# Squaring each block right behind its clipping on ScalarE, in the feed-forward stages of a fused transformer kernel

## The reference

```
def squared_relu_mlp(h, w1, w2):
    return jnp.square(jax.nn.relu(h @ w1)) @ w2
```

## Time and profile before

| | us |
|---|---|
| median of 3 runs | 3998.24 (3997.82 to 4001.41) |
| the profiled execution, its own time | 3994.2 |
| its span, first to last instruction | 3992.4 |
| TensorE matmul busy | 3734.4 (94%) |
| TensorE weight load busy | 3000.8 (75%) |
| VectorE busy | 1972.5 (49%) |
| ScalarE busy | 1335.9 (33%) |
| GpSimd busy | 807.8 (20%) |

### The profile page before, as it was taken

The page is one execution under the profiler, slowest core; times in us unless marked ns, Lnnn a source line. Parts: engine busy times, 40 slices in busy tenths (PEclk is TensorE's granted clock), DMA queues, the critical chain, the costliest instruction groups (busy, mean ns, idle before and its releaser), DMA issues. The chain is left out here.

```text
span 3992.4 us, 54790 instructions
## 1 busy us (share of the span) xinstructions
PE 3734.4 (94%) x20683; PEld 3000.8 (75%) x20683; DVE 1972.5 (49%) x2905; ACT 1335.9 (33%) x2365; POOL 807.8 (20%) x604
## 2 busy tenths in 40 slices
PE   6998899999999899999999999999989988899998
PEld 4775688888878677777776688888878865577886
DVE  5736643333353564333446663333356638746445
ACT  3346532121243454222335422121233324433222
POOL 1500012222122111222220012222110018701222
PEclk9999999999999999999999999999999989999999
DMA  5134223233221212444310023233211230032222
GB/s 177 64 116 127 64 85 120 91 112 109 86 73 63 76 42 85 153 152 149 106 55 1 12 89 124 87 118 103 91 56 63 76 118 14 19 106 94 92 91 71
DMA packets 191734, 352.34 MB, mean 88 GB/s; under 512 B 41980, under 2 KB 43597, under 8 KB 191565
## 3 DMA queue, kind: packets, MB, share of 16 engines
q1 hardware_dynamic: 183789, 333.48, 25.5%
q10 hardware_dynamic: 7792, 16.78, 1.1%
HBM read 341.71 MB, written 16.92 MB: 90 GB/s over the span
## 5 line engine op out<-in xcount | busy, mean ns | idle before, releaser
L568 POOL TENSOR_TENSOR x<-x,scaled_buf 128x512 f32<-128x512 f32 (+1 forms) x360 | 465.3, 1298 | 2296.6 <-DVE scaled_buf L560 2295.9
L129 DVE TENSOR_TENSOR w_lo<-raw,w_hi 128x2048 fp32r<-128x2048 f32 x198 | 459.1, 2319 | 789.3 <-ACT w_hi L123 774.9
L123 ACT ACTIVATE w_hi<-raw 128x2048 fp32r<-128x2048 f32 x197 | 377.1, 1914 | 1206.3 <-PE psum L385 1203.9
L383 PE MATMUL psum<-hT_hi,w_hi 128*128 128x256 f32 (+1 forms) x1920 | 677.8, 353 | 3.1 <-issue 1.7
L384 PE MATMUL psum<-hT_lo,w_hi 128*128 128x256 f32 (+1 forms) x1920 | 674.5, 351 | 0.0
L385 PE MATMUL psum<-hT_hi,w_lo 128*128 128x256 f32 (+1 forms) x1920 | 674.1, 351 | 0.0
L383 PE MATMUL psum<-w_hi,uT_hi 128*128 128x512 f32 x1280 | 505.7, 395 | 17.7 <-DVE uT_lo L639 17.7
L560 DVE TENSOR_TENSOR scaled_buf<-psum,gate 128x512 f32<-128x512 f32 x360 | 246.6, 690 | 512.3 <-PE psum L385 478.7
L385 PE MATMUL psum<-w_hi,uT_lo 128*128 128x512 f32 x1280 | 499.3, 390 | 0.0
L384 PE MATMUL psum<-w_lo,uT_hi 128*128 128x512 f32 x1280 | 498.9, 390 | 0.0
L383 PE MATMUL psum<-w_hi,hT_hi 128*128 128x512 f32 x1072 | 420.6, 392 | 9.3 <-ACT qkv L1232 5.9
(11 more groups left out here) (277 smaller groups left out, 4742.9 us busy)
## 6 DMA issues: line engine op xcount, KB each, us to landing
mod_wide<-in_w_mod SPq DMA_DIRECT2D x24, 3072.0 KB, 10.6
raw<-in_w_mlp SPq DMA_DIRECT2D x64, 1024.0 KB, 5.2
raw<-in_ff_w SPq DMA_DIRECT2D x64, 1024.0 KB, 5.3
raw<-in_ssm_w_in SPq DMA_DIRECT2D x20, 1024.0 KB, 5.1
mod_slab<-in_w_mod SPq DMA_DIRECT2D x8, 2048.0 KB, 8.0
raw<-in_b_w_qkv SPq DMA_DIRECT2D x12, 1024.0 KB, 5.1
raw<-in_a_w_qkv SPq DMA_DIRECT2D x11, 1024.0 KB, 5.1
mod_first<-in_w_mod ACTq DMA_DIRECT2D x4, 2048.0 KB, 17.0
```

The source lines that it names most:

```text
L123: act.activation(K.w_hi[h][:, :, :], K.raw[h][:, :, :], ACT.Copy).then_inc(K.hi_done.h, 1)
L129: dve.tensor_tensor(K.w_lo[h][:, :, :], K.raw[h][:, :, :], K.w_hi[h][:, :, :].bitcast(F32), ALU.subtract).then_inc(K.lo_done.h, 1)
L383: pe.matmul(out, hi_a, hi_w, start=first, stop=False, **check)
L568: pool.tensor_tensor(x, x, K.scaled_buf[:, j % 2, :], ALU.add).then_inc(K.added.h, 1)
```

## The change

The squaring of bank j is issued directly behind the clipping of bank j. Before, it was issued behind the clipping of bank j+1 (and the last one behind the squaring ahead of it). The same instructions with the same waits remain; their order on ScalarE changes from clip 0, clip 1, square 0, clip 2, square 1, ... to clip 0, square 0, clip 1, square 1, ...

```
                     tile_done(act, c, 0, j)
                     act.wait_ge(K.sq_done.h, sq0 + nt * c + j - 1)
                     act.activation(K.relu[:, j % 2, :], K.bank[j][:, :], ACT.Relu).then_inc(K.relu_done.h, 1)
-                    if j:
-                        square(c, j - 1)
-                square(c, nt - 1)
+                    square(c, j)
                 split_hi(K, act, g + 1, 1)
```

## The result

| | us |
|---|---|
| before, median of 4 runs | 3998.03 |
| with the change, median of 4 runs | 3974.38 (3972.85 to 3976.63) |
| ratio | 0.9941, 95% interval 0.9929 to 0.9953 |
| profiled execution, own time, before and after | 3994.2 and 3973.86 |
| its span, before and after | 3992.4 and 3972.0 |

The kernel is 0.59% faster, 23.6 us in the medians (18.8 to 28.4 by the interval), 20.3 us between the two profiled executions. Forecast were 22.2 us and a time of 3976.0 with a range of 3969 to 3986.

The account below looks back on a forecast made before the run. TensorE, running matmuls 94% of the span, was taken to bound the kernel, stalling for block 2 in sixteen chunks. Removing 16 x 1.386 = 22.2 us from the median 3998.24 gave 3976.0 us, 8-in-10 range 3969 to 3986.

Parts of the forecast that it names:

- The place: Sixteen chunks of the stages without context: TensorE waits for block 2 of `uT_lo`; stages with context: cost and gain 0.
- The cause: On ScalarE, square 2, data ready since 1636.81, stands behind clipping 3, which waits for bank 3, and starts at 1639.43.
- The size: TensorE in each stalled chunk: 1.386 us lost by matmul starts, 1.41 by chunk length; 16 x 1.386 = 22.2 us.
- The two counts by idle time: TensorE's wait for `uT_lo`: 17.7 us by matmul rows, 24.4 by weight loads, taken to bracket the stall's size.
- What is late next: Stages without context: block 3 reaches TensorE at 1641.42, is wanted at 1642.75, so 1.3 us to spare.
- the cover: Down-projection start: 18 matmuls, k = 0 to 2 of two tiles, 4.1 us, hide the line's 2.8 us.
- The hand-over from a clipping to its square: ScalarE, from a clipping's end to its dependent square: 0.03 us, with 0.1 as the other end.
- The slab half and the first gating: VectorE: half 1's subtraction over at about 1644.4, wanted at 1649.5; first gating waits for it, at no cost.
- The slower rival: ScalarE loses its clip-square overlap, 0.13 x 160 = 21 us, and becomes the pace: 4019 us; chance 3%.
- The new wait of a square for VectorE: ScalarE: a square waits for VectorE's block j-2 ahead of the next clipping; square 2 has 3.4 us to spare.
- Given back in part: Shift against reduced-clock dips, or block 3 later than worked out, leaves half the gain: 3987 us; chance 7%.
- the shift that the rival spoke of: All that follows the shortened chunks moves by 11 and 22 us against the clock's dips; part of the 7% rival.

Follow-up runs that it names:

- fivefold square: New order, with square 3 computed five times in the sixteen chunks without context tokens, against the kernel before: 3995.79 us, ratio 1.0001.
- taking the cover away: New order, but TensorE takes all four products of output tiles 0 and 1 at once, against the kernel before: 3985.33 us, ratio 0.9974.
- the fourth experiment: ScalarE in old order; TensorE takes k = 0 and 1 of output tiles 0 and 1 before k = 2, against the kernel before: 3976.80 us, ratio 0.9949.

## Why the prediction was right

- *The place.* TensorE waits for block 2, in the sixteen chunks of the stages without context, and nowhere else. Shown: the new order there alone gives all, with context tokens it gives nothing, and square 2 alone gives all.
- *The cause.* Square 2 stood behind clipping 3, whose data came later. Shown twice, from both sides: by moving that square and by letting TensorE ask later.
- *The size.* 1.386 us a chunk by starts, 1.41 by the length of six chunks. Measured 1.41 by the chunks' length (44.935 to 43.52), 22.6 us for sixteen. The medians moved by 23.6, the profiled executions by 20.3; both hold 22.2 within what runs of one kernel differ by (3.8 us among the four of the changed one). The two counts by idle time, 17.7 and 24.4, would have been off by 4.9 and 1.8 us from the chunks' length: the matmul rows leave out the slow step behind a gap and part of the gap itself.
- *What is late next.* Block 3, with 1.3 us to spare, from the rows of before. In the profile after it is 1643.08 - 1641.73 = 1.35, less 0.05 on the way. The fivefold square gives 1.31, and taking the cover away exposed the line at the size worked out (0.74 us late, 0.7 expected).
- *The hand-over from a clipping to its square* was taken as 0.03 us with 0.1 as the other end. Both occur: 0.03 (1636.56 to 1637.19) and 0.11 (1633.84 to 1634.55). It touched nothing, since both fit in the idle 1.38 us ahead of the next clipping.
- *The slab half and the first gating.* VectorE's subtraction of the half ends at 1642.38 + 2.29 = 1644.67, that is 5.67 us behind the start of the down-projection, where 5.7 were worked out (1644.4 against 1638.66). TensorE had no wait from it. The first gating does stand behind it, as forecast, and starts at 1644.59. In its sum for the end of tile 0 the prediction counted one step too many: the 21st matmul starts 20 steps in, so the end was due at 1643.6 and not 1643.8, which changes nothing else.
- *The slower rival*, ScalarE's lost overlap: it is lost (19 us more busy time, 21 were worked out) and nobody waits for it. The new wait of a square for VectorE showed once in 160, 0.4 us.
- *Given back in part.* Net 2.2 us, outside the sixteen chunks, are of this kind. The mean granted clock was 0.979 against 0.980. The 1.8 us ahead of the second stage go with a stretch of reduced clock that the profile before doesn't have. This stretch lies before the first shortened chunk, so it isn't the shift that the rival spoke of. What makes up the 1.4 and 1.0 us between the later stages stays open; all three lie within the spread of the runs.

## What to carry to other kernels

On an engine that executes in order, an instruction whose data is ready can stand behind one whose data isn't: software pipelining by one step (clip 1 ahead of square 0) saves that engine a tenth of a microsecond and delays its consumer by a whole bank. It is wrong where the engine is idle and somebody waits for its result, as here; where the engine itself is the bottleneck it may be right, which no run here tested. Look then for the last link only: the gain stops where the next late block comes in, and how far off that is can be worked out from starts in the timeline before the change is made.

To size a stall on TensorE, compare starts with the undisturbed step, or the length of a whole chunk with matmuls times step; the idle times shown ahead of the rows are too small for the matmuls (17.7 us here, where 22.6 were lost) and too large for the weight loads (24.4).

## What the runs showed of the hardware

- After a wait of TensorE for `uT_lo` that shows 0.6 to 1.2 us of idle time, the second matmul comes 0.34 us behind the first, not 0.227, at a granted clock of 1.00. Such a gap costs 0.11 us more than its own length, in all sixteen chunks that stall of the kernel before, of the fivefold square and of the one without the cover. With the rest of a stall in the fourth experiment (0.05 us a chunk) no step between matmuls of the down-projection's first tiles is longer than 0.25 us in the chunks looked at.
- The distance from a clipping to its dependent square is 0.63 us in some places and 0.71 in others, by position: in the second stage banks 0 and 1 have 0.71 and banks 2 and 3 have 0.63 in every chunk but the last, in the fourth stage banks 0 to 2 have 0.71, and in the last chunk of each stage, which is written out behind the loop, all have 0.63. The cause is open; that it lies in how the waits come out in the loop's code is a guess that wasn't tried.
- Each square took 0.632 us instead of 0.623 when it came directly behind the clipping that it depends on. The same 0.632 show in the fivefold square, where an extra square waits for the one directly ahead of it.
- Short stretches of reduced clock move about from kernel to kernel. In the kernel with square 2 alone one fell on the start of the fourth stage (granted clock 0.91 from 3610 to 3630 us), and the first clippings of the stage's first two chunks, at 3618.97 and 3664.13, are 45.16 us apart instead of 43.52.
